# Three fp32r passes for every weight unit and both expert tables, split in quarters by VectorE and GpSimd, with the row sums kept in h0

## The reference

```python
z = h @ w_in[l]                                     # q | k | v | conv B | conv C | conv h | two gates
attn = sliding_window_sink_attention(q, k, v, sinks[l]) @ w_attn_out[l]
conv = (cb * causal_short_conv(cc * ch, conv_w[l])) @ w_conv_out[l]
merged = gates[..., :D_MODEL] * attn + gates[..., D_MODEL:] * conv
h = layer_norm(ALPHA * h + merged @ w_o[l], ln1_g[l], ln1_b[l])
# peer_ffn(h): 8 heads x 16 experts of 16384 for each token
q = (xt @ w_q).reshape(t_, PEER_HEADS, 2, PEER_HALF)          # scores, top 16 x top 16, top 16
u = jnp.take(u_tab, ec, axis=0)
act = jax.nn.gelu(jnp.einsum('cd,chkd->chk', xc, u), approximate=False)
v = jnp.take(v_tab, ec, axis=0)
y = jnp.einsum('chk,chkd->cd', gc * act, v)
h = layer_norm(ALPHA * h + y, ln2_g[l], ln2_b[l])
```

## Time and profile before

| | us |
|---|---|
| median of 3 runs (lowest to highest) | 4401.99 (4394.59 to 4404.37) |
| profiled execution, its own time | 4392.56 |
| its span | 4390.7 |

### The profile page before, as it was taken

The page is one execution under the profiler, slowest core; times in us unless marked ns, Lnnn a source line. Parts: engine busy times, 40 slices in busy tenths (PEclk is TensorE's granted clock), DMA queues, the critical chain, the costliest instruction groups (busy, mean ns, idle before and its releaser), DMA issues.

```text
span 4390.7 us, 57764 instructions
## 1 busy us (share of the span) xinstructions
PE 4025.5 (92%) x22327; PEld 3582.0 (82%) x22327; DVE 2502.2 (57%) x3128; ACT 974.2 (22%) x1140; POOL 947.5 (22%) x568
## 2 busy tenths in 40 slices
PE   7899999998878999999998999698889899999997
PEld 7789999997756788888887788587778787777886
DVE  3444455446867654545655895665556535666555
ACT  3444333333212200000000000011111003333332
POOL 0000000002444333323442234432234420100000
PEclk9999999998989899999999999899999999999999
DMA  4234544543498898788998789998889986877664
GB/s 164 89 122 172 192 173 177 186 172 143 190 357 340 314 383 350 310 325 342 415 383 321 270 330 426 384 383 318 334 328 369 424 341 258 304 298 277 226 241 164
DMA packets 174570, 1239.88 MB, mean 282 GB/s; under 512 B 15408, under 2 KB 48256, under 8 KB 61056
## 3 DMA queue, kind: packets, MB, share of 16 engines
q1 hardware_dynamic: 74496, 663.83, 39.2%
q0 software_dynamic: 73728, 536.90, 31.3%
q10 hardware_dynamic: 26240, 37.75, 2.3%
HBM read 1200.68 MB, written 37.75 MB: 282 GB/s over the span
## 4 chain that ended last, share of the span: by engine, by line
PE 66%; DMA 12%; DVE 8%; issue 6%; ACT 4%; ACTq 2%; POOL 1%; SPq 0%; DVEq 0%; POOLq 0%
PE dense_ps L837 31%; PE dense_ps L823 7%; PE dense_ps L825 7%; PE dense_ps L824 7%; DMA row<-in_peer_u_dram,cols 5%; PE dense_ps L1027 4%; DMA e_gate<-gate_spill 4%; DMA gate_spill<-gbuf 3%; PE dense_ps L868 3%; PE score_ps L1027 2%; PE o_ps L924 2%; ACTq L685 2%; PE score_ps L992 1%; DVE row L1065 1%; ACT mT L561 1%
## 5 line engine op out<-in xcount | busy, mean ns | idle before, releaser
L837 PE MATMUL dense_ps<-xT,wbuf 128*128 128x256 f32 x7808 | 1722.1, 382 | 21.7 <-ACT stage L682 20.0
L837 PEld LDWEIGHTS dense_ps<-xT,wbuf 128*128 128x128 f32 x7808 | 1491.3, 192 | 230.8 <-ACT stage L682 20.4
L455 POOL DMA_INDIRECT row<-in_peer_v_dram,cols x256 | 439.7, 1718 | 1195.1 <-DVE y L1070 1125.7
L1070 DVE SCALAR_TENSOR_TENSOR y<-row,wgt,y 128x2048 f32<-128x2048 f32 x256 | 601.5, 2349 | 147.6 <-DMA row<-in_peer_v_dram,cols 131.3
L1065 DVE SCALAR_TENSOR_TENSOR row<-row,h 128x2048 f32<-128x2048 f32 x256 | 581.5, 2288 | 134.1 <-DMA row<-in_peer_u_dram,cols 130.7
L455 POOL DMA_INDIRECT row<-in_peer_u_dram,cols x256 | 417.0, 1629 | 735.0 <-DVE row L1065 683.1
L1118 DVE TENSOR_TENSOR w_lo<-wbuf,w_hi 128x2048 fp32r<-128x2048 f32 x153 | 350.5, 2292 | 386.5 <-ACT w_hi L487 386.3
L823 PE MATMUL dense_ps<-act_hi,w_hi 128*128 128x256 f32 x1856 | 533.9, 288 | 6.7 <-DVE w_lo L1118 4.9
L824 PE MATMUL dense_ps<-act_lo,w_hi 128*128 128x256 f32 x1856 | 530.0, 286 | 0.0
L825 PE MATMUL dense_ps<-act_hi,w_lo 128*128 128x256 f32 x1856 | 529.9, 286 | 0.0
L1502 DVE TENSOR_TENSOR v_lo<-wbuf,v_hi 128x2048 fp32r<-128x2048 f32 x128 | 293.1, 2291 | 326.7 <-ACT v_hi L736 326.7
(11 more groups left out here) (202 smaller groups left out, 4648.3 us busy)
## 6 DMA issues: line engine op xcount, KB each, us to landing
wbuf<-in_w_units_dram SPq DMA_DIRECT2D x230, 2048.0 KB
wbuf<-in_peer_v_dram SPq DMA_DIRECT2D x64, 2048.0 KB
act_spill<-stage ACTq DMA_DIRECT2D x64, 256.0 KB
gate_spill<-gbuf ACTq DMA_DIRECT2D x4, 4096.0 KB, 43.1
e_act<-act_spill SPq DMA_DIRECT2D x32, 512.0 KB, 8.7
e_gate<-gate_spill SPq DMA_DIRECT2D x32, 512.0 KB, 9.6
cT<-in_x_dram SPq DMA_DIRECT2D x2, 2048.0 KB, 11.2
row<-in_peer_u_dram,cols POOLq DMA_INDIRECT x256
```

The source lines that it names most:

```text
L455: pool.indirect_dma_start(out=row[j % RING][:, :], out_offset=None, in_=tab[:, :], in_offset=bass.IndirectOffsetOnAxis(ap=cols[:, c, j:j + ...
L837: last = nc.tensor.matmul(dense_ps[n % 4][:, c, :], wbuf[n % 2][:, k, c * P:(c + 1) * P], src[:, k, :], start=(k == 0), stop=(k == KT - 1))
L1070: V.scalar_tensor_tensor(out=y[:, :], in0=row[slot][:, :], scalar=wgt[:, bass.ds(col, 1)], in1=y[:, :], op0=ALU.mult, op1=ALU.add).then_in ...
```

## The change

- Every unit, of both halves and both tables, is multiplied in three fp32r passes. The plain fp32 path is gone.
- A unit is split in four quarters of 128 x 1024. ACT makes the high quarter in one shared `w_hi` of four quarters; the low quarter is written in place over the weights in `wbuf`. Quarters 1 and 3 are subtracted by GpSimd, quarters 0 and 2 by DVE; near the two PQ stages (`POOL_ALL`) all four by GpSimd.
- A weight load is two DMAs of 1 MB, each started as its half of the buffer has been used.
- The rows' dots of both token tiles come first, then all sums. `y` is gone: the sum is kept in `h0`. The ring has 3 rows in place of 4. How many rows stand in a unit is a table (`rows_in`): 0 to 3, and 3 in every `peer_v` unit until all 512 are used.
- The gate table is written in eight chunks of 32 tokens, with two `gbuf` in turn.
- The loops of DVE, ACT and POOL are written out.

```diff
-GCHUNK = 64
+GCHUNK = 32
...
-RING = 4
...
+RING = 3
...
+POOL_ALL = (range(U_PQ, UNITS + U_Q + 1), range(UNITS + U_PQ, N_U + 8))
+def by_pool(n, j):
+    return j % 2 == 1 or any(n in r for r in POOL_ALL)
+def rows_in(n):
+    r, j, m = n - UNITS, n - N_U, n - N_V
+    if m >= 0:
+        return 3
+    if j >= 0:
+        return 0 if j < 4 else 1 if j < 8 else 2 if G_FIRST <= j < G_FIRST + 32 else 3
+    if r < U_Q or r >= U_PQ:
+        return 0
+    if r < U_GA:
+        return 2
+    if r < U_CONV:
+        return 3
+    if r < U_GC:
+        return 3 if r % 3 == 2 else 2
+    return 3
...
-        wbuf = [sb(f"wbuf{i}", [P, KT, UC]) for i in range(2)]
+        wbuf, wbuf_at = zip(*(at(f"wbuf{i}", [P, 4, 1024]) for i in range(2)))
+        w_hi = sb("w_hi", [P, 4, 1024], F32R)
...
+        w_lo = [over(wbuf_at[i], f"w_lo{i}", [P, 4, 1024]) for i in range(2)]
...
+            def low(n, j):
+                pool.wait_ge(w_hi_ready, 4 * n + j + 1)
+                nc.gpsimd.tensor_tensor(w_lo[n % 2][:, j, :], wbuf[n % 2][:, j, :], w_hi[:, j, :].bitcast(F32), ALU.subtract
+                                        ).then_inc(lo_by_pool, 1)
...
+            for n in range(N_V + U_UNITS):
+                for j in range(4):
+                    if by_pool(n, j):
+                        low(n, j)
+                    if n > UNITS + U_Q and j % 2:
+                        upto = ROWS_TO[n - 2] + RING - (rows_in(n - 2) // 2 if j == 1 else 0)
+                        for g in range(sent, min(upto, ALL_ROWS)):
+                            gather(g)
+                        sent = max(sent, min(upto, ALL_ROWS))
...
+            def split_hi(n, j, per=0, i=0):
+                if n and j < 3:
+                    act.wait_ge(quarter_used, (3 * per) * i + (3 * n + j - 2))
+                if n and j == 3:
+                    act.wait_ge(dense_ready, per * i + n)
...
+                act.activation(w_hi[:, j, :], wbuf[n % 2][:, j, :], ACT.Copy).then_inc(w_hi_ready, 1)
...
+            for m in range(U_UNITS):
+                n = N_V + m
+                if m + 2 < U_UNITS:
+                    split_lo(n + 2, 0)
+                rows(n, 0, 2)
+                if m % 2 == 0 and m + 4 < U_UNITS:
+                    e_mult(m // 2 + 2)
+                if m % 2 and m + 3 < U_UNITS:
+                    e_rest((m + 3) // 2)
+                if m + 2 < U_UNITS:
+                    split_lo(n + 2, 2)
+                rows(n, 1, 2)
```

More of the change, by code:

```diff
@@ L505, in _ @@
                 n0 = UNITS * b
-                with_rows = b == 1 and OVERLAP
                 move_transposes(2 * b)
-                first = b == 0
-                if first:
-                    split_hi(0, 0)
-                    split_hi(0, 1)
+                if not b:
+                    for j in range(4):
+                        split_hi(0, j)
+                for j in range(3):
+                    split_hi(n0 + 1, j)
                 if b:
@@ L1045, in _ @@
+            for m in range(U_UNITS - 4, U_UNITS):
+                unit_V(m, t_outer=m == U_UNITS - 1)
         @block.vector
@@ L1084, in finish_tile, with rows, finish_stats @@
+            def rows(n, part=0, parts=1):
+                if n < UNITS:
+                    return
+                first, count = ROWS_TO[n - 1], ROWS_TO[n] - ROWS_TO[n - 1]
+                for g in range(first + count * part // parts, first + count * (part + 1) // parts):
+                    take(g)
+            def finish_stats(t):
+                dve.wait_ge(row_used, U_ROWS + SLOTS * (t + 1) + START)
                 for c in range(4):
-                    V.bn_stats(bst2[:, c, :], y[:, c * 512:(c + 1) * 512]).then_inc(fin_step, 1)
@@ L1128, in _ @@
             for b in range(HALVES):
-                rows_on = b == 1 and OVERLAP
-                first = b == 0
-                if first:
+                n0 = UNITS * b
+                if not b:
                     split_transposes(0)
-                    for q in range(9):
-                        split_lo(q)
-                else:
-                    Rows(rows_on, 0, 0, 0, 0).use(16)
-                with dve.Fori(0, 2) as i:
-                    rows = Rows(rows_on, 0, 0, 32, i, base=16)
+                for n in range(n0, n0 + 5):
+                    split_unit(n)
+                for i in range(2):
                     for u in range(4):
@@ L1314, in _ @@
[L1314 to L1321 removed]
+                for c in range(8):
+                    n = n0 + U_OUT + c
+                    to = hs[b][:, :, c * UC:(c + 1) * UC]
+                    dve.wait_ge(dense_out, n + 1)
+                    V.scalar_tensor_tensor(out=to, in0=to, scalar=ALPHA, in1=stage[n % 4][:, :, :],
+                                           op0=ALU.mult, op1=ALU.add).then_inc(out_step, 1)
+                    split_lo(n + 2, 0)
+                    rows(n, 0, 2)
+                    if c % 2:
+                        dve.wait_ge(out_step, 8 * b + c + 1 + START)
+                        for t in range(TILES):
+                            V.bn_stats(bst[:, t, c // 2, :], hs[b][:, t, (c - 1) * UC:(c + 1) * UC]
+                                       ).then_inc(stats_step, 1)
+                    split_lo(n + 2, 2)
+                    rows(n, 1, 2)
@@ L1434, in _ @@
                 k = 1
-                rows = Rows(rows_on, 1, 0, 0, 0, base=16)
+                if not b:
+                    split_transposes(2)
                 for t in range(TILES):
@@ L1452, in _ @@
                         k += 1
-                        rows.use(2)
-                    if first:
+                    if not b:
                         dve.wait_ge(gather_step, f + k)
```

922 lines of the change are left out of this document (364 added, 558 removed).

## The result

| | before | after |
|---|---|---|
| median (lowest to highest) | 4403.18 (4394.59 to 4410.68), 4 runs | 4848.32 (4846.99 to 4852.06), 4 runs |
| span of the profiled execution | 4390.7 | 4845.2 |
| mean granted TensorE clock, of 2.4 GHz | 0.959 | 0.903 |

The changed kernel is slower: the ratio is 1.1013, with a 95% interval of 1.0992 to 1.1034, or 445 us. The prediction was 4465 us, in a range of 4110 to 4560. Its direction was right, its size was not.

What follows compares the result with a forecast made beforehand. PE was taken to bound the kernel before; after, DVE and POOL taking turns from GA on. Stage terms summed to 4380 us, plus 80 us of loss made 4460 of span, given as 4465 us, range 4110 to 4560.

Steps and rivals of the forecast that it cites:

- The turns: Half 1: POOL subtractions and two-operand DVE instructions wait for each other's end; chance 0.52 with a loss, 0.13 without gap.
- The sum per unit: DVE's two-operand work plus POOL's subtractions per unit: GA and convolution 13.9 us, GC 14.3, placing 14.2, peer_v 15.4.
- the prediction's bracket: Convolution, seven rows to three units: (15.4 + 7.2 + 13.8 + about 5)/3, given as 13.9 us a unit.
- the 2 and the 9 us: Added roughly to the 4460 us span: profiled run 2 us longer than its span and 9 us under the median.
- no turns: Two-operand DVE work runs beside POOL's subtractions, so PE or DMA decides: 4076 us, chance 0.20.
- turns in part: DVE is held for only a piece of each POOL subtraction, say half: 4150 to 4350 us, chance 0.15.
- the clock as a cause of its own: PE at granted clock 0.85: an 11.5 us unit takes 13.5, still under 13.9; upper end only, no chance given.
- Hidden at no cost: ACT's 4.2 us a unit, SP's smaller DMAs (8.6 us for 1 MB each) and the written-out loops' instructions add nothing.
- The loss of 80 us: Gaps in the shared read path from GA on: 3% of 2680 us, with bounds of nothing and about 6%.
- The prediction's own sign of a larger loss: A GA unit over 15.5 us with the durations standing would mean the loss is under-sized, by the ring of three.
- The spill waits: ACT's waits for the gate spill in the U units, about 125 us, go with two buffers of 32 tokens.
- Rival 1: No turns; PE or DMA decides, 12.4 us a three-row unit, 13.6 in peer_v (905 in all): 4076 us, chance 0.20.

Runs made afterwards that it cites:

- e8: e1 with the quarters and rows of GA and GC alternating, GpSimd keeping half of the subtractions; 4456.96 us median, 1.0132 of before.
- e9: e8 with ACT's activation write behind a gate chunk issued a unit later, behind that unit's high parts, and its last-chunk wait four units later; 4390.13 us, 0.9961 of before.
- e1: The changed kernel with each load of e in peer_v issued on SP ahead of two weight loads, not behind them; 4511.98 us median, 1.0273 of before.
- e3: e2 with each row sum over only 64 columns, so DVE's row work is nearly gone; 4174.54 us, one run.
- e2: e1 with each of the 512 row instructions replaced by a one-operand reduce over the row; 4256.98 us, one run.
- e4: e1 with DVE subtracting all four quarters from the second GA unit of half 1 on, apart from the POOL_ALL ranges; 4408.91 us median, 1.0039 of before.
- e10: e6 with the same two ACT edits as e9 (later activation write behind a gate chunk, later last-chunk wait); 4172.35 us median, 0.9470 of before.
- e6: e4 with GA/GC quarters and rows alternating, quarter 3 subtracted in the next unit's work, and rows spread over attention, U and peer_v; 4249.43 us, 0.9655 of before.

## Why the prediction went wrong

**What held.** *The turns.* The step from two gathers and one copy to "a POOL subtraction and a DVE instruction with two SBUF operands take turns" was right, in the direction that no row had shown: 124 rows waited for the whole rest of a subtraction, and as a reduce over one operand none did. Its ground was weaker than it looked: the copy of the earlier trace rows has one input, so it is not the case of two inputs, and it was held all the same, as the copies of the changed kernel are. By the Trainium skill (SBUF — State Buffer, section "Who interferes with whom") a DVE instruction with two SBUF inputs contends with GpSimd's reads, and the trace agrees: 2.74 and 2.79 us a row on average in the changed kernel, 3.88 where it began inside a subtraction, 2.28 without the second operand. *The sum per unit.* The convolution was forecast at 334 us for 24 units and took 332 (the terms in the prediction's bracket give 13.8 us a unit, not 13.9, which is 2 us less; and 4460 with the 2 and the 9 us that it adds at the end is 4471, not 4465). GA was forecast at 13.9 us a unit and takes 14.0 in e8, where only the order is mended. U with placing was forecast at 14.2 and takes 14.5 to 15.0 in e9. `peer_v` was forecast at 1013 and takes 996 in e8. So no turns and turns in part fell by the durations, and the clock as a cause of its own, since it fell in the stages where PE waited (0.81 in `peer_v`) and rose with the wait gone (0.91).

**The step that failed.** "Hidden at no cost: [...] the smaller DMAs of SP (each has three quarters of a unit, 8.6 us, for 1 MB)". The load of e is on SP too, behind two weight loads, before and after. The change makes the second of them wait for PE in place of DVE. It was given no term at all: DVE waited 430.3 us for it, where it had waited 24.9, and e1 shows 340 us of time (1331 to 991). The mechanism can be read off the code: `load_e` keeps its place, and the wait ahead of it goes from `v_lo_ready` to `dense_ready`. The prediction looked at how much room each load has, and not at what stands in front of it in SP's one line. With this term the prediction would have been 4380 + 340 + 80 = 4800 us of span, 1% under the 4845.

**The loss of 80 us** was of about the right size for what remains (4454 in e8, and 74 over the sum) but of another kind, so its agreement proves little. The prediction's own sign of a larger loss came, a GA unit of over 15.5 us (241 us for 15 units is 16.1), but it laid that to the ring of three, and DVE waited less for rows than before. What e8 and e9 show in its place are two more orders:
- GA and GC: quarters in one block ahead of the rows. 241 to 210 and 263 to 236 us, 58 in all, of which e1 to e8 gives 53.
- U: "The spill waits (about 125 us [...]) go as well" was wrong. Before, ACT waited for a chunk itself three times; behind the fourth the next write of 256 KB was held, and this was in the trace of before and in no term:

```profile
3371.89 0.41 ACTq L706 DMA_DIRECT2D gate_spill<-gbuf  x1
...
3385.06 73.55 ACTq L685 DMA_DIRECT2D act_spill<-stage  x1
```

  Now every chunk but the last does this, 71.1 us in seven times, and ACT waits 17.3 once for the last. That is 65 of U's 89 us over the forecast in the units with placing (540 to 475).

With these three mended, e9's profiled span is 4398 us and its median 4390, against a sum of 4380 without a loss. The stages still differ singly: the attention took 189 us, 31 less than forecast, and half 0 with its end 22 less; PQ took 20 more, because the eight units that make the scores take 13.5 us each but the transposes ahead of them were counted too short; the rest of U 19 more. These were not taken apart by a run. So the closeness of the sum is in part a balance of errors of both signs. The direction, too, was right in part by luck: the sum without a loss is no slower than the kernel before, and e9, with the three orders mended, has 0.9961 of it.

**Rival 1 in the end.** It had the DMA bound right in kind: with the rows' work all but left out (e3), `peer_v` takes 919 us for the 905 of that rival. Taking the turns away alone (e2, e4) does not reach its 4076 us; e10, without turns and with all orders mended, has 4172.

## What to carry to other kernels

An issue in a queue's line comes no earlier than the waits ahead of it allow, and a change to one of those waits moves it though its own line stays: write down, for each issue of SP, which unit's end the instructions ahead wait for and at which unit the taker stands in line, and compare the two. Where one engine prepares parts for PE and does other work too, let the two alternate in its code in the pieces in which PE releases the buffers. And before an edit is costed by busy time, look at whether two engines' instructions can run side by side at all; a row of the very instruction that began inside the other's tells it, and one of another instruction may not: a reduce and a copy, each with one input, behaved differently here.

## What the runs showed of the hardware that was not expected

- A product of DVE with two SBUF operands that begins inside a POOL subtraction (128 x 1024, 2.35 us) does all of its work behind it: it ends some 2.15 us after it, in 124 of 127 cases. A `tensor_reduce` over the same row is not held (2.285 us in 160 cases). A copy with one input is (2.36 us for 0.16, in ten cases).
- The issue of a gather on POOL is held by a row product too. It took 0.94 us where it began inside a `tensor_reduce` (63 cases in e2), and 2.75 us on average where it began inside a row product of the changed kernel (some 200 cases).
- The issue of a write on ACT's queue is not free when a large one is ahead. Behind a 2 MB write of `gbuf`, the issue of 256 KB held ACT for 10.1 us in the changed kernel, and for up to 19.3 us in e6, where the DMA engines are busier (336 GB/s in that stage); 29 us after the large write it took 0.4 us again in e9, but at that distance up to 3.7 us in e10. Behind the last write of 4 MB in the kernel before it held for 73.55 us. Why the queue holds was not measured.
- The DMA engines were full at different rates: share 0.98 at 395 GB/s in `peer_v` of e3, 1.01 at 423 GB/s before. A bound from the fullest window of another stage was 6% too low here (13.6 us for a `peer_v` unit, 14.4 measured).
- In the stretches where PE waited, its mean granted clock (a share of 2.4 GHz, over times at 2.4 and at 1.2) was lower: 0.81 in `peer_v` and 0.87 in GA of the changed kernel. With the waits mended and the same matmuls it was 0.91 (e1) and 0.94 (e8) there, and 1.00 in the placing stage of e9.
